# A fused encoder layer on one core: the front's blocks turned at once, the zero store moved into attention, PSUM banks dealt by age, and the second transposition ahead of a piece

## The reference, cut to what matters

```python
mod = silu(c) @ ada_w + ada_b                 # six parts of 1024: shift, scale, gate, twice
h = rms_norm(x, norm1_g) * (1 + sc1) + sh1
proj = h @ w_in                               # q, k, v | mlstm q, k, v, o, gates | branch gates
attn = windowed_gqa(rope(q), rope(k), v, sink)
qk = silu(centred_dwconv(proj[mlstm q, k]))
hm = rms_norm(h_fw + h_bw)                    # mlstm in both directions, per head
mlstm_out = sigmoid(o) * hm
merged = bg1 * (attn @ w_up_attn) + bg2 * (mlstm_out @ w_up_mlstm)
x = x + g1 * (merged @ w_out)
h2 = rms_norm(x, norm2_g) * (1 + sc2) + sh2
x = x + g2 * moe(h2)                          # 4 groups, top-1; 16 experts, top-2; gated MLP 1024-512-1024
y = rms_norm(x, final_norm_g)
```

## Time and profile before

| | |
|---|---|
| median of 3 timed runs | 821.04 us (819.28 to 822.76) |
| the profiled execution | 825.5 us, its span 823.5 us (2.0 us lie outside the span) |
| granted TensorE clock, mean | 0.936 of full |
| PE busy | 719.3 us, 87% of the span |
| DVE, ACT, POOL busy | 517.1, 395.9, 199.1 us |
| moved by DMA | 192.22 MB, 233 GB/s over the span |

### The profile page before, as it was taken

How to read it: one execution, slowest core, us unless ns; L and a number is a source line. 1 busy time by engine, 2 the same in 40 slices (tenths; PEclk the granted TensorE clock), 3 DMA queues, 4 the chain that set the end, 5 groups by cost and what they waited for, 6 DMA issues and landing times.

```text
span 823.5 us, 9855 instructions
## 1 busy us (share of the span) xinstructions
PE 719.3 (87%) x3662; PEld 571.9 (69%) x3662; DVE 517.1 (63%) x655; ACT 395.9 (48%) x487; POOL 199.1 (24%) x107
## 2 busy tenths in 40 slices
PE   4689996999999999998998499999999999999810
PEld 3456674667787887887887477887787877777610
DVE  2425562260345544785508889888888888888637
ACT  5323112142446274423313258667777777766523
POOL 1003223233232231356741101221121222200030
PEclk9779997999999999999999579999999999999965
DMA  9980686566721311466621588999999999994253
GB/s 317 305 221 8 201 318 223 197 204 185 226 78 27 102 52 52 166 208 229 263 68 47 199 346 348 373 382 377 371 373 385 383 372 387 375 359 170 105 198 134
DMA packets 78591, 192.22 MB, mean 233 GB/s; under 512 B 14350, under 2 KB 55574, under 8 KB 72412
## 3 DMA queue, kind: packets, MB, share of 16 engines
q1 hardware_dynamic: 71172, 169.86, 58.7%
q0 software_dynamic: 4272, 11.31, 3.9%
q10 hardware_dynamic: 3112, 10.59, 3.2%
HBM read 179.10 MB, written 16.83 MB: 238 GB/s over the span
## 4 chain that ended last, share of the span: by engine, by line
PE 42%; DVE 27%; issue 15%; ACT 9%; DMA 4%; POOL 1%; ACTq 1%; SPq 1%; POOLq 0%; DVEq 0%
PE psum L811 32%; DVE moe_low L2207 13%; ACT half_high L1509 3%; ACT xbuf L1422 2%; DVE xsT_low L2217 2%; PE psum L881 2%; ACT xbuf L1430 2%; DMA front_ring<-w_in 2%; PE psum L1059 1%; PE psum L895 1%; DVE xbuf L1844 1%; DVE slot L1776 1%; PE psum L915 1%; DVE stat L1849 1%; DVE oT L2226 1%
## 5 line engine op out<-in xcount | busy, mean ns | idle before, releaser
L2321 POOL TENSOR_TENSOR low_ring<-front_ring,high_ring 128x1024 fp32r<-128x1024 f32 x50 | 121.6, 2436 | 295.2 <-ACT high_ring L1328 295.2
L1328 ACT ACTIVATE high_ring<-front_ring 128x1024 fp32r<-128x1024 f32 x52 | 54.9, 1056 | 188.8 <-PE psum L811 144.8
L2207 DVE TENSOR_TENSOR moe_low<-front_ring,half_high 128x2048 fp32r<-128x2048 f32 x48 | 107.9, 2285 | 10.0 <-ACT half_high L1509 10.0
L811 PE MATMUL psum<-half_high,xsT_low 128*128 128x512 f32 x256 | 103.9, 406 | 9.4 <-DVE xsT_low L2217 9.4
L811 PE MATMUL psum<-h_low,high_ring 128*128 128x512 f32 x288 | 111.3, 405 | 0.0
L811 PE MATMUL psum<-h_high,low_ring 128*128 128x512 f32 x224 | 94.1, 420 | 16.3 <-DVE h_low L1703 8.1
L811 PE MATMUL psum<-half_high,xsT_high 128*128 128x512 f32 x256 | 101.9, 398 | 0.0
L811 PE MATMUL psum<-moe_low,xsT_high 128*128 128x512 f32 x256 | 101.7, 397 | 0.0
L1509 ACT ACTIVATE half_high<-front_ring 128x2048 fp32r<-128x2048 f32 x48 | 90.9, 1914 | 6.3 <-PE psum L811 6.0
L811 PE MATMUL psum<-h_high,high_ring 128*128 128x512 f32 x224 | 90.5, 404 | 0.0
L2207 DVE TENSOR_TENSOR moe_low<-slots,half_high 128x2048 fp32r<-128x2048 f32 x32 | 73.0, 2285 | 8.6 <-ACT half_high L1509 8.6
(11 more groups left out here) (301 smaller groups left out, 1279.0 us busy)
## 6 DMA issues: line engine op xcount, KB each, us to landing
front_ring<-w_down SPq DMA_DIRECT2D x16, 2048.0 KB, 10.6
front_ring<-w_in SPq DMA_DIRECT2D x34, 512.0 KB, 5.4
xbuf<-ada_w SPq DMA_DIRECT2D x32, 512.0 KB, 5.0
slot<-w_gate SPq DMA_DIRECT2D x8, 2048.0 KB, 9.3
front_ring<-w_up SPq DMA_DIRECT2D x8, 2048.0 KB, 9.2
slots<-w_up SPq DMA_DIRECT2D x8, 2048.0 KB, 9.4
slots<-w_gate SPq DMA_DIRECT2D x8, 2048.0 KB, 9.4
y_rows<-inout ACTq DMA_DIRECT2D x16, 512.0 KB, 8.9
```

The costliest lines, as they stand in the source:

```text
L811: mm = pe.matmul(out, lhs(a, k), rhs(b, k), start=(start and k == 0 and a == 1), stop=(stop and k == count - 1 and (a, b) == (0, 0)))
L1328: act.activation(dst, src.rearrange("p (k n) -> p k n", k=KD), ACT.Copy).then_inc(high_ready, 1)
L2207: dve.tensor_tensor(low_of(slot, h), half_of(slot, h), half_high[place].bitcast(F32), ALU.subtract).then_inc(low_dve, 1)
L2321: pool.tensor_tensor(low, src, high.bitcast(F32), ALU.subtract).then_inc(low_ready, 1)
```

## The change

It reorders work, moves one store, and deals banks anew. No product is added or left out.

1. *Front.* PE does block 0 after two turned parts of x, and turns its rows after four. Each later block is multiplied as soon as the chain of the one before is under way, its rows are turned after three or six matmuls, and products whose h is older fill the time (`columns_out` with other ranges). ACT and DVE take the last parts of x later, DVE splits the second piece behind the turned rows of block 1.
2. *Zeros.* POOL clears `modrow` (128 x 512) instead of a part of `hm`, after the split of piece `bg1,2` and when the last two `ada` parts are in DRAM; SP stores the 4 MB from it behind the load of `bg2,0`, in attention. ACT, no longer DVE, waits for the end of that store, ahead of the third half weight of the experts.
3. *Forget gates.* Exp and Ln at `mk2`, the scans at `mv0`.
4. *Banks.* In the projections the table begins at bank 5, so that each product takes the bank that was emptied earliest; `mv`, `mo` and the `ada` parts get other banks; `w_out` and the router take the eight banks of the groups just before, oldest first.
5. *Merge.* `mT0` to `mT3` stand ahead of piece `upa3` on PE, ACT and DVE.
6. *`w_out`.* The last piece, `wo1,3`, is split into a place of its own (`last_split`) and no longer waits for a slot of the split ring.

```diff
@@ list_groups
+    turned = lambda *ks: [(f"xT{k}", "sv"[k % 2]) for k in ks]
+    g = [("cT", "s"), ("gainT", "v")] + turned(0, 1) + [("first0", "v")] + turned(2, 3) + [("column0", "v")]
+    g += turned(4, 5, 6, 7)
...
-    g += [(f"upa{j}", "v") for j in range(KD)]
+    g += [(f"upa{j}", "v") for j in range(6)]
     g += [(f"mT{t}", "v") for t in range(TT)]
+    g += [(f"upa{j}", "v") for j in range(6, KD)]
@@ banks
-BANK.update({name: n for name, _, n in ROUTER})
-BANK.update({name: 6 + int(name[3:]) % 2 for name in PROJECTED if name.startswith("ada")})
-BANK.update({name: n % 6 for n, name in enumerate(n for n in PROJECTED if not n.startswith("ada"))})
-BANK.update({"turn4": 5, "gateT": 5, "mv0": 0, "mv1": 1, "mv2": 2, "mv3": 3,
-             "mo0": 4, "mo1": 6, "mo2": 0, "mo3": 1})
+BANK.update({name: 7 - int(name[3:]) % 2 for name in PROJECTED if name.startswith("ada")})
+BANK.update({name: (n + 5) % 6 for n, name in enumerate(n for n in PROJECTED if not n.startswith("ada"))})
+BANK.update({"turn4": 5, "gateT": 5, "mv0": 0, "mv1": 1, "mv2": 3, "mv3": 4,
+             "mo0": 2, "mo1": 7, "mo2": 0, "mo3": 1})
+OLDEST = [BANK[name] for name, _ in GROUPS[INDEX["wo0.0"] - BANKS:INDEX["wo0.0"]]]
+BANK.update({name: OLDEST[n % 2 * TT + n // 2] for name, _, n in ROUTER})
+BANK.update({"rank": 0, "ids": 1, "ids_more": 7})
@@ split parts
+        last_split = [placed_over("last_high", "rot_pT", 4096, [P, PIECE])[:, :],
+                      placed_over("last_low", "oT", 0, [P, PIECE])[:, :]]
...
-            pair = first_split[n if piece in FIRST_PIECES else n % SPLIT_SLOTS]
+            pair = last_split if piece == SPLITS[-1] else first_split[n if piece in FIRST_PIECES else n % SPLIT_SLOTS]
@@ SP
-                if piece == ("mk", 0):
+                if piece == ("bg2", 0):
                     sp.wait_ge(zeros_ready, 1)
                     sp.dma_start(y_rows[2 * MIN_PAIRS * P:2 * MAX_PAIRS * P, :]
...
@@ PE, after the first four turned parts
             columns_out(to_keys, range(0, 1))
             turn_block(1)
             columns_out(to_keys, range(1, 2))
             columns_out(to_values, range(0, 2))
             first_block(2)
             columns_out(to_keys, range(2, 3))
             turn_block(2)
             columns_out(to_keys, range(3, 4))
             columns_out(to_values, range(2, 4))
             columns_out(to_query0, range(0, 2))
             first_block(3)
             columns_out(to_query0, range(2, 4))
             turn_block(3)
             columns_out(to_keys, range(4, 6))
             columns_out(to_values, range(4, 6))
             columns_out(to_query0, range(4, 6))
             columns_out(to_query1, range(0, 6))
...
-            for j in range(4):
+            for j in range(3):
                 widen(("upa", j), o_parts)
             for t in range(TT):
                 pe.wait_ge(hm_ready, t + 1)
                 transposes(f"mT{t}", [hm[:, t, k * P:(k + 1) * P] for k in range(KM)])
+            widen(("upa", 3), o_parts)
             wait_emptied(pe, "mT3")
@@ ACT
-                if what == ("mv", 0):
+                if what == ("mk", 2):
...
-            for n in range(6):
+            for n in range(5):
                 next_high((f"wo{n % 2}", n // 2))
+            split_high(len(SPLITS) - 1)
@@ DVE
-                elif what == ("mv", 2):
+                elif what == ("mv", 0):
                     gate_scans()
...
-                if u == 0:
-                    dve.wait_ge(zeros_stored, 16)
@@ POOL
-            pool.memset(hm[:, 2:4, :], 0.0).then_inc(zeros_ready, 1)
...
+                if piece == ("bg1", 2):
+                    for s in (2, 3):
+                        pool.wait_ge(row_stored[s], 16 * 4)
+                    pool.memset(modrow[:, :, :], 0.0).then_inc(zeros_ready, 1)
```

More of the change, by code:

```diff
@@ L175, in list_groups @@
 def list_groups():
-    g = [("cT", "s"), ("gainT", "v")] + [(f"xT{k}", "sv"[k % 2]) for k in range(4)]
-    g += [("first0", "v"), ("xT4", "s"), ("xT5", "v"), ("column0", "v"), ("xT6", "s"), ("xT7", "v")]
+    turned = lambda *ks: [(f"xT{k}", "sv"[k % 2]) for k in ks]
+    g = [("cT", "s"), ("gainT", "v")] + turned(0, 1) + [("first0", "v")] + turned(2, 3) + [("column0", "v")]
+    g += turned(4, 5, 6, 7)
     for n in range(1, FIRST_BLOCKS):
@@ L736, in _ @@
                 load_piece(piece)
-                if piece == ("mk", 0):
+                if piece == ("bg2", 0):
                     sp.wait_ge(zeros_ready, 1)
                     sp.dma_start(y_rows[2 * MIN_PAIRS * P:2 * MAX_PAIRS * P, :]
-                                 .rearrange("(s p) d -> p s d", p=P),
-                                 hm[:, 2:4, :].rearrange("p a b -> p (a b)").rearrange("p (s d) -> p s d", s=1)
-                                 .to_broadcast([P, 2 * (MAX_PAIRS - MIN_PAIRS), D])).then_inc(zeros_stored, 16)
+                                 .rearrange("(p s) (h n) -> p (s h) n", p=P, n=COLS),
+                                 modrow[:, :, :].rearrange("p (a s) n -> p a (s n)", a=1)
+                                 .to_broadcast([P, 4 * (MAX_PAIRS - MIN_PAIRS), COLS])).then_inc(zeros_stored, 16)
                 for s in range(4):
@@ L936, in _ @@
             pe.wait_ge(xn_ready, TT)
-            for k in range(4):
-                turn_tokens(k)
[L939 to L944, removed]
+            turn_tokens(0)
+            turn_tokens(1)
+            first_block(0)
+            turn_tokens(2)
+            turn_tokens(3)
+            turn_block(0)
+            for k in range(4, KD):
+                turn_tokens(k)
             to_keys, to_values, to_query0, to_query1 = FIRST_PIECES
-            columns_out(to_keys, range(0, 2))
             first_block(1)
+            columns_out(to_keys, range(0, 1))
+            turn_block(1)
+            columns_out(to_keys, range(1, 2))
             columns_out(to_values, range(0, 2))
-            turn_block(1)
-            columns_out(to_keys, range(2, 4))
+            first_block(2)
+            columns_out(to_keys, range(2, 3))
+            turn_block(2)
+            columns_out(to_keys, range(3, 4))
             columns_out(to_values, range(2, 4))
-            first_block(2)
-            columns_out(to_query0, range(0, 4))
-            turn_block(2)
+            columns_out(to_query0, range(0, 2))
+            first_block(3)
+            columns_out(to_query0, range(2, 4))
+            turn_block(3)
             columns_out(to_keys, range(4, 6))
             columns_out(to_values, range(4, 6))
-            first_block(3)
             columns_out(to_query0, range(4, 6))
-            turn_block(3)
             columns_out(to_query1, range(0, 6))
@@ L1352, in _ @@
             empty_tokens(4)
-            empty_tokens(6)
             for n in range(4):
@@ L1356, in _ @@
                 make_h(2 * n + 1)
+                if n == 0:
+                    empty_tokens(6)
                 if n < 3:
@@ L1395, in _ @@
                     act.activation(rows_x, rows_x, ACT.Ln, bias=1.0).then_inc(forget_ln, 1)
-                elif name == "aq":
+                if name == "aq":
                     copy_raw(j + 1)
@@ L1473, in _ @@
                                bank(f"mT{t}").rearrange("p (k t) -> p k t", k=KM), ACT.Copy).then_inc(mT_high, 1)
+            next_high(("upa", 3))
             for j in range(4):
@@ L1545, in _ @@
             act.wait_ge(h2_stored, 16 * TT)
+            act.wait_ge(zeros_stored, 16)
             high_half(None, 2, UP, 0, 1)
@@ L1725, in _ @@
             empty_tokens(1)
+            empty_block(0)
             empty_tokens(3)
-            empty_block(0)
             low_first(0)
+            block_turned(0)
             empty_tokens(5)
-            block_turned(0)
-            empty_tokens(7)
             for n in range(FIRST_BLOCKS):
@@ L1734, in _ @@
                 split_h(2 * n + 1)
[L1735 to L1738, removed]
+                if n == 0:
+                    empty_tokens(7)
+                elif n < 3:
+                    low_first(n + 1)
                 if n + 1 < FIRST_BLOCKS:
                     empty_block(n + 1)
+                    block_turned(n + 1)
                     if n == 0:
                         low_first(1)
-                    block_turned(n + 1)
             link(dve.memset(ones_row, 1.0))
@@ L1966, in _, with gate_attention @@
             wait_emptied(dve, "bg15")
-            for j in range(KD):
+            def gate_attention(j):
                 wait_full(dve, f"upa{j}")
@@ L1970, in _ @@
                                                  in1=bank(f"upa{j}"), op0=ALU.add, op1=ALU.mult))
+            for j in range(6):
+                gate_attention(j)
             for t in range(TT):
@@ L1976, in _ @@
                                           m_parts[0][:, :, own].bitcast(F32), ALU.subtract))
+            for j in range(6, KD):
+                gate_attention(j)
             def merge(j):
```

## The result

The changed kernel takes 789.88 us, the median of 4 runs (789.26 to 790.24); the kernel before took 820.55 beside it (4 runs, 819.28 to 822.76). The ratio is 0.962, 95% interval 0.9585 to 0.9655: faster, by 30.7 us. The forecast was 787.0, range 780 to 797. The profiled execution took 790.24 us, its span 788.4, the mean granted clock 0.955 (before 825.5, 823.5 and 0.936).

A forecast was written before the change was run, and what follows sets the result against it. Ahead of the experts PE was taken to set the pace, so only its waits and half clock could be won: 9.0 + 14.0 + 7.4 + 3.6 = 34.0 off the median of 821.04 gives 787.0 us, range 780 to 797.

The forecast's parts named there:

- Front, 9.0: Front: PE's waits for the split of h and half clock go, blocks 2 and 3 start as loads land; 9.0 us.
- The rival of the chain: Front: bound by its chain, not by the loads, with waits for h moving elsewhere; gives 3, so 793 us; chance 0.08.
- Zero store, 10.0 of the 14.0: Projections: PE's waits and half clock behind the zero store go, 10.0 us; 14.0 includes the last piece.
- The wait for `ada_w`: Projections: PE's wait for this load, counted to the zero store, goes with the move; 2.5 us.
- Banks and scans, 7.4: Projections to first scores: waits of 1.3, 1.9, 1.2 and 1.4 go, with 1.6 of half clock; 7.4 us.
- the 1.6 of clock at `mv0`: Projections: the 24 matmuls of `mv0` take 5.71 instead of 7.32 us; 1.6.
- 1.4 for the scans: Projections: scans two pieces earlier leave DVE free for `ada4`, so PE's wait there goes; 1.4 us.
- Merge and last piece, 3.6 and 4.0: Merge: a wait and half clock go, net 3.6 us. `w_out`: the wait ahead of `wo1,3` and half clock go, 4.0.
- The 34.0: Whole kernel: the sum 9.0 + 14.0 + 7.4 + 3.6, taking the span from 823.5 to 789.5 us.
- The four clock terms (7.4): Half clock behind waits at the zero store, last piece, `mv0` and merge: 2.4, 1.8, 1.6, 1.6; 7.4 us together.
- The clock was won back: Answers the rival that smaller remaining waits still lose the clock in four terms: 794.4 us, chance 0.12.
- That the experts take the gain in: Experts: rival that their load stream is the bound, so the end stays at 816 to 821 us; chance 0.03.

The follow-up runs named there:

- before_again: The kernel before, profiled once more with no edit: 817.49 us.
- front_back: The changed kernel with the front's order of before on PE, ACT and DVE: 798.97 us, ratio 0.9749 to the kernel before.
- zeros_alone: The kernel before with only the zero store moved into attention: 810.74 us, ratio 0.9895 to the kernel before.
- The second store: The changed kernel with 4 MB more of zeros stored, into rows that the experts write later: 800.46 us, ratio 0.9754 to the kernel before.
- before: The first profile of the kernel before, without the change: profiled execution 825.5 us, span 823.5.
- banks_back: The changed kernel with the banks of before, the scans staying early: 795.02 us, ratio 0.9695 to the kernel before.
- banks_scans_back: The changed kernel with both the banks and the scans of before: 795.76 us, ratio 0.9724 to the kernel before.

## Why the prediction held, and where it was off

**Front, 9.0.** Right in size by the median (9.1) and against its own profile (9.6), and in its working: block 2 starts at 34.50 (34.1 forecast) behind its load, block 3 at 42.65 (41.9 to 43.1), and the end at 60.23 lies in the stated 59.3 to 60.5. The rival of the chain is out: no wait on h is left. But the 69.8 that it starts from is one execution's: in the three other profiles with the old order (`before_again`, `front_back`, `zeros_alone`) the front ends at 65.9, 66.0 and 65.5, which leaves 5.3 to 5.8 of it. That the median still comes to 9.1 is not explained by these profiles, and agreement to 0.1 is more than prices known to 2.5 us can show.

**Zero store, 10.0 of the 14.0.** 8.8 and 8.5 measured. The wait for `ada_w` was over-counted. In attention it costs nothing, as taken: the piece behind it is 1.5 us late on ACT instead of 5.8 (287.4 less 281.62), and 3.3 of this difference is the store, which lands that much sooner than assumed. The second store shows how near the edge that is.

**Banks and scans, 7.4.** 5.9 measured together, 8.5 by the ratios. The waits came back one by one as listed (1.3, 1.9, 1.4, 1.2 are 5.8); the 1.6 of clock at `mv0` is paid in some executions. The split within the term was wrong: 1.4 for the scans holds only while the banks are old.

**Merge and last piece, 3.6 and 4.0.** 4.8 measured together instead of 7.6, 6.5 by the ratios. Waits and half clock are there, and put PE 6.6 us back ahead of the experts. The experts' stage is 2.0 shorter in that profile; whether it answers the delay or differs by itself stays open.

**The step that was mis-sized** is the last line of the sum, "The median of the timed runs is 4.5 lower than the profiled one, 821.04: less 34.0 gives 787.0". The 34.0 was read from an execution that paid for the clock in every place that the sum counts, and so was longer than any of the 37 timed runs of the kernel before (825.5 against 823.15 at most). The four clock terms (7.4) and some 4 us within the front belong to that execution; the median pays part of them, and is lower for that very reason. Taken off it in full, they are counted twice. The 33 timed runs of the kernel before in the experiments bear it out: the three shortest (814.87 to 815.77) have a granted clock of 0.947, the seven longest (822.61 to 823.15) one of 0.936 to 0.938, and the profiled execution has 0.936. Against its own execution the sum holds to 1.1 us: 789.5 forecast for the span, 788.4 measured. The median of the changed kernel lies 0.4 under its profiled execution, not 4.5. The medians of the four groups of parts, 9.1 + 8.8 + 5.9 + 4.8, make 28.6 of the 30.7; by the ratios they make 36, so that the shares are known less well than the whole.

**The rivals.** The clock was won back in all four places that the sum counts; it is lost in a new one, where block 2 takes 3.55 behind a wait of 4.1, and that had been allowed for in the front. The Trainium skill (TensorE: Matmul & The Clock Gate, Part 1) has the point of release differ between runs of one kernel. The two executions of before agree that the clock differs between runs: of the 8.0 us between them 7.1 are clock behind the same waits. That the experts take the gain in is out: from the product of the gathered rows to the end the span takes 349.4 us before and 349.3 after.

## What to carry to other kernels

Work out a sum on the profiled execution, then ask which of its terms every execution pays: here PE's waits for another engine mostly repeated to a tenth of a microsecond (those for a load did not: 2.1 to 4.4 ahead of block 2), the half clock behind a wait of 2 to 3 us did not, and the profile above all timed runs had paid it in every place that the sum counts. Two stalls in a row on one engine are one stall when the same late engine stands behind both: take them away together, and price them together. A transfer put under a stage that has spare bandwidth is free up to the slack of the first load queued behind it: here the 3.4 us from that piece being split to its use by PE.

## What the runs showed of the hardware

The granted clock behind equal waits of PE differs between executions. Behind the 1.9 us ahead of `mv0`, 24 matmuls took 7.32, 7.33 and 7.30 us in three profiles (`before`, `zeros_alone`, `banks_back`) and 5.70 in two (`before_again`, `banks_scans_back`); behind the 2.4 us at the merge, 48 took 12.75, 12.59, 12.77 and 12.78 in four and 11.20 in one. Behind 4.7 to 4.8 us it fell each time (8.15, 8.33 and 8.06 for 24).

With those waits gone, the scatter of the time is smaller too, as far as four runs tell: the changed kernel's lie within 1.0 us, the four of the kernel before beside them within 3.5, and all 37 of it within 8.3. With the banks or the scans alone taken back, six runs lie within 5.2 and 6.2.
